# The last layer's output norm moved into its attention, with a new order of the attention's steps

## The chip, the cores and the metric
The kernel runs on one core of one Trainium2 chip. The metric is device time in microseconds (us) of one execution. The core has five engines that matter here: PE (TensorE, matrix products and transposes), ACT (ScalarE), DVE (VectorE), POOL (GpSimd) and SP (SyncE), which issues every DMA in order. They run side by side and wait for each other through semaphores.

## The reference
Two layers of an encoder, for a prompt of 1024 rows (eight tiles of 128) and a sample of 32 rows (tile 8, `SMP`), each row of 1024 features, all in float32.

```
for each layer:
    h = rms_norm(x, g_norm)
    queries, keys, values, gate, index queries/keys/weights = h @ w_in (parts are rotated)
    A: index score = sum over 4 index heads of weight * relu(iq . ik); the 256 best keys a row;
       8 heads of attention over those keys (2 groups of 4 heads)
    B: 4 heads over a window of the last keys, with a sink
    M: 4 heads over 256 memory rows
    x = x + (concat(A, B, M) * silu(gate)) @ w_out
y = rms_norm(x, g_final)
```

The keys and values of each layer are outputs too.

## The kernel before
Python builds one list, `STEPS`, and each engine walks it and issues its own part of each step, so the list is the order of work on every engine. A layer has these stages.

- **Keys and index.** For each tile t: `KEYS` projects, `NORM` transposes the normed rows of tile t+2, `KEYS_T` transposes the keys, and `INDEX` steps score tile t-2. An `INDEX` step before is a pair of index heads on up to 512 keys: two products, each in one half of PE's rows, into a buffer of 1024 columns (L837). ACT applies relu to each half (L1053), and DVE adds each, with its sign, to `bias` (L1320, L1322). There are two score buffers, `score_ps`, and two for transposes, `turn_ps`, used in turn. The sample has 1056 keys, so it takes six steps.
- **Queries and gate**, with the search for the 256th best score in 32 `COUNT` steps on DVE (L1253) and ACT (L969).
- **Attention.** For each tile, four items: B, A group 0, M, A group 1. An item has `QK` steps (scores; DVE adds the mask and takes the maximum, ACT exponentiates, L1099 and L1113), then groups of up to four 128-wide blocks. Two groups make a batch: two `PT` steps (PE transposes the probabilities, L731; ACT, L1124, or DVE, L1444, copies them), then the `PV` products of the batch before. `MIX` (L1460) multiplies by the gate. `OUT` (L746, two halves of 512 columns, 16 records each) projects the mixed tile t-1 during tile t, and `ADD` (L1474) adds it to the residual in `x_sb`, which has two buffers. The order is written out by `attention_steps`; a tile t from 1 to 7 has t+3 batches.
- M scores (and B's of the sample) are read by ACT straight from the score buffer ("direct"); A's and the other B's are first written to SBUF by DVE.
- **Masks.** DVE turns a tile's index scores into a mask in two blocks, `need_of_tile` and `mask_tile`, each beside an `OUT`.
- **The gate's divisors.** From tile 1 on the sums of the softmax are divided out in the gate. `SCALE` (DVE, L1414) makes the reciprocals; SP writes them to DRAM (L682, "norm write"), waits, and loads them back spread over the partitions (L689); POOL multiplies the gate by them (`GATE_SCALE`, L1154); `MIX` waits for that.
- SP's queue in the attention, in order, for t = 1 to 8: norm turn of t for B and M, norm turn of t for A, store of tile t-1 (L696), loads of tile t+1, the residual rows and the gate (L672, L673).
- **The last block**, behind a barrier: all nine tiles are loaded from DRAM, squared and summed on ACT (L1509), mean and power on POOL (L1517, L1520), multiplied on DVE (L1529) and stored.

Of the kernel before, what the change touches and what calls it, by code (L numbers as in the profile page):

```python
# [13 lines left out]
P = 128  # L14
# [36 lines left out]
OUT_AT = [[("A", 0, 1), ("A", 1, 0)], [("A", 0, 1)]]  # L51
# [51 lines left out]
def attention_steps():  # L103


    steps, late, waiting, held, last_mixes = [], [], [], [], []
    last_group = (len(ITEMS) - 1, len(groups_of(ITEMS[-1])) - 1)

    def finish():

        pv = late.pop(0)
        i, g = pv[1:]
        t, kind, kv = ITEMS[i]
        out = [pv]
        if g == len(groups_of(ITEMS[i])) - 1:
            if kind == "M":
                out.append(("MIX", t, 1))
            elif (kind, kv) == ("A", 1):
                out.append(("MIX", t, 0))
        return out  # L120
# [8 lines left out]
    steps += [("EXTRA",)] + score_steps(1)  # L129
    waiting += divisors(score_steps(1)[-1])  # L130
    for i, it in enumerate(ITEMS):
        nxt = score_steps(i + 2) if i + 2 < len(ITEMS) else []
        groups, given = len(groups_of(it)), 0
        t = it[0]
        for g in range(groups):

            if t and it[1:] + (g,) in OUT_AT[t == SMP]:
                c = OUT_AT[t == SMP].index(it[1:] + (g,))
                steps.append(("OUT", t - 1, c))
                if t + 1 in SEARCHED:  # L140
                    steps.append(("MASK", SEARCHED.index(t + 1), c))
                steps.append(("ADD", t - 1, c))
            made = []
            while given < len(nxt) and given * groups <= g * len(nxt):
                steps.append(nxt[given])
                made += divisors(nxt[given])
                given += 1
            if g == groups - 1:
                for q in nxt[given:]:
                    steps.append(q)  # L150
                    made += divisors(q)


            if t == 0 and g == 0:
                steps.append(("DIVIDE", i))
            held.append(("PT", i, g))
            if len(held) == 2 or (i, g) == last_group:
                steps += held
                mixes, last_mixes = last_mixes, []
                steps += mixes  # L160
                while late:
                    for s in finish():


                        (last_mixes if s[0] == "MIX" and s[2] else steps).append(s)
                late += [("PV",) + s[1:] for s in held]
                held.clear()
            if g == 0:
                steps += waiting
                waiting.clear()  # L170
            waiting += made
    steps += last_mixes
    while late:
        steps += finish()
    return steps + [s for t, c in ((NT - 1, 1), (SMP, 0)) for s in (("OUT", t, c), ("ADD", t, c))]
# [9 lines left out]
def index_steps(t):  # L185

    return [("INDEX", t, hp, c) for hp in range(IDX_HEADS // 2) for c in range(-(-NKEYS[t] // 512))]


def plan():  # L190

    steps = [("SQUARE", 0), ("SQUARE", 1), ("NORM", 0), ("NORM", 1)]
    for t in range(TILES):

        index = index_steps(t - 2) if t - 2 in SEARCHED else []
# [59 lines left out]
def copied_by_dve(a):  # L255

    return a % 5 in (1, 3)
# [1318 lines left out]
```

## Time and profile before

| what | value |
|---|---|
| median of 3 runs | 1604.13 us (1602.92 to 1609.43) |
| profiled execution, its own time | 1599.02 us |
| its span | 1597.2 us |
| PE busy | 1400.2 us, 88% |
| DVE busy | 920.6 us, 58% |
| ACT busy | 657.4 us, 41% |
| POOL busy | 155.9 us, 10% |
| mean granted clock of PE | 0.949 |

The span is what the profiler records, and the time is a little longer. Shares are means over stages with different limits, so they are read stage by stage. In the rows, "[1.86 <-DVE hT L1285]" means that the engine was idle for 1.86 us before the instruction, and that DVE's write of `hT` at line 1285 ended the wait. A group "x4" is four records run together; one float32 product of this kernel leaves two records.

### The profile page before, as it was taken

How to read it: one execution, taken by the hardware profiler on the slowest of the kernel's cores; microseconds unless marked ns; L12 is line 12 of the kernel's file. 1: busy time of each engine (PE TensorE's matmuls, PEld its weight loads, DVE VectorE, ACT ScalarE, POOL GpSimd, SP SyncE). 2: the span in 40 equal slices, each digit the busy share in tenths (PEclk: the TensorE clock that was granted, in tenths of full speed). 3: DMA queues.
4: the chain of work that ended last, by engine and by line, in shares of the span. 5: the costliest groups of instructions: out<-in, count | busy, mean ns of one | idle time of the engine just before them, and what ended most of it. 6: DMA issues, size and time to landing. Idle time of an engine off the chain costs nothing. (4 is left out here: it accounts for less than half of the span.)

```text
span 1597.2 us, 19488 instructions
## 1 busy us (share of the span) xinstructions
PE 1400.2 (88%) x6364; PEld 778.1 (49%) x6364; DVE 920.6 (58%) x2527; ACT 657.4 (41%) x1667; POOL 155.9 (10%) x187
## 2 busy tenths in 40 slices
PE   5988799999889999988599887999997999998881
PEld 3444356666545444444344343666664444544450
DVE  1444636887656677655133446488775557676533
ACT  1123526776634433333111334377655333344332
POOL 1100013300001000000011001132000001000003
PEclk9999999999989999999689998999998999999976
DMA  6100410123132312111241004003124222111106
GB/s 200 53 25 21 156 47 1 45 88 94 67 88 73 80 53 54 26 35 29 62 160 52 25 18 161 27 0 119 35 86 133 54 57 57 54 47 53 34 4 247
DMA packets 117960, 108.58 MB, mean 68 GB/s; under 512 B 52368, under 2 KB 90992, under 8 KB 117872
## 3 DMA queue, kind: packets, MB, share of 16 engines
q1 hardware_dynamic: 117872, 107.45, 22.1%
q8 instruction: 51, 0.84, 0.2%
q14 instruction: 37, 0.30, 0.1%
HBM read 81.76 MB, written 25.76 MB: 67 GB/s over the span
## 5 line engine op out<-in xcount | busy, mean ns | idle before, releaser
L746 PE MATMUL score_ps<-w_slot,hT 128*128 128x512 f32 (+2 forms) x1024 | 391.9, 542 | 12.5 <-ACT prob_bm L1053 7.6
L746 PEld LDWEIGHTS score_ps<-w_slot,hT 128*128 128x128 f32 x1024 | 197.7, 196 | 193.3 <-issue 187.3
L746 PE MATMUL score_ps<-w_slot,work 128*128 128x512 f32 x512 | 234.6, 612 | 5.5 <-issue 5.4
L1099 ACT ACTIVATE hT<-hT,neg_top 128x128 f32<-128x128 f32 (+8 forms) x144 | 116.8, 812 | 288.0 <-DVE neg_top L1372 287.8
L1253 DVE TENSOR_SCALAR_CACHE_REDUCE work<-bias,trial 128x384 f32<-128x384 f32 (+3 forms) x256 | 226.1, 883 | 6.9
L969 ACT ACTIVATE work<-bias,neg_trial 128x768 bf16<-128x768 f32 (+2 forms) x192 | 198.4, 1043 | 67.3 <-DVE neg_trial L1249 67.3
L746 PEld LDWEIGHTS score_ps<-w_slot,work 128*128 128x128 f32 x512 | 97.5, 196 | 129.8 <-issue 129.6
L817 PE MATMUL score_ps<-hT,w_slot 128*128 128x352 f32 x448 | 135.2, 460 | 1.4 <-ACT gate_raw L1083 1.4
L731 PE MATMUL turn_ps<-ident,hT 128*128 128x128 f32 (+1 forms) x720 | 98.9, 277 | 27.6 <-ACT work L1124 17.2
L1154 POOL TENSOR_TENSOR work<-work,norm_sb 128x512 f32<-128x512 f32 (+1 forms) x32 | 38.9, 1216 | 855.7 <-DMA norm_sb<-norm_scratch 855.7
L871 PE MATMUL score_ps<-akT,query_mem 64*128 64x512 f32 (+4 forms) x448 | 103.1, 547 | 9.4 <-ACT prob_bm L1113 6.5
L731 PEld LDWEIGHTS turn_ps<-ident,hT 128*128 128x128 f32 (+1 forms) x720 | 74.5, 147 | 74.0 <-issue 33.2
L817 PEld LDWEIGHTS score_ps<-hT,w_slot 128*128 128x128 f32 x448 | 84.8, 190 | 48.4 <-issue 1.7
L1354 DVE CUSTOM_DVE_ANT_0 hT<-score_ps,bias 128x512 f32<-128x512 f32 (+4 forms) x144 | 80.8, 598 | 42.9 <-PE score_ps L871 42.4
L1021 ACT COPY work<-score_ps 128x64 f32<-128x64 f32 (+2 forms) x112 | 20.5, 300 | 179.0 <-PE score_ps L746 179.0
L1124 ACT COPY work<-turn_ps 128x512 f32<-128x512 f32 (+1 forms) x102 | 56.6, 570 | 81.9 <-PE turn_ps L731 81.9
L1474 DVE TENSOR_TENSOR gate_raw<-score_ps,gate_raw 128x512 f32<-128x512 f32 x32 | 22.1, 692 | 118.1 <-PE score_ps L746 118.1
L1320 DVE TENSOR_SCALAR bias<-prob_bm,iw_sign 128x512 f32<-128x512 f32 (+5 forms) x26 | 12.9, 496 | 125.8 <-ACT prob_bm L1053 125.5
L927 PE MATMUL out_a_ps<-work,a_v_sb 128*64 128x256 f32 (+1 forms) x560 | 73.7, 382 | 0.0
L731 PE MATMUL turn_ps<-ident,prob_bm 128*128 128x128 f32 (+2 forms) x280 | 43.3, 286 | 34.3 <-ACT work L1124 24.5
L731 PE MATMUL turn_ps<-ident,work 128*128 128x128 f32 (+1 forms) x284 | 44.3, 292 | 32.8 <-DVE hT L1285 14.9
L1322 DVE SCALAR_TENSOR_TENSOR bias<-prob_bm,iw_sign,bias 128x512 f32<-128x512 f32 (+5 forms) x78 | 51.6, 661 | 29.1 <-ACT prob_bm L1053 26.9
(179 smaller groups left out, 1768.2 us busy)
## 6 DMA issues: line engine op xcount, KB each, us to landing
w_slot<-in_w_in_dram SPq DMA_DIRECT2D x8, 2048.0 KB, 10.3
gate_raw<-in_x_prompt_dram SPq DMA_DIRECT2D x16, 512.0 KB, 3.7
work<-gate_scratch SPq DMA_DIRECT2D x16, 512.0 KB, 4.7
x_scratch<-gate_raw SPq DMA_DIRECT2D x16, 512.0 KB, 4.6
gate_raw<-x_scratch SPq DMA_DIRECT2D x16, 512.0 KB, 3.5
norm_sb<-norm_scratch SPq DMA_DIRECT2D x56, 128.0 KB, 4.1
gate_scratch<-gate_raw SPq DMA_DIRECT2D x16, 264.0 KB, 3.1
gate_scratch<-gate_raw SPq DMA_DIRECT2D x8, 528.0 KB, 2.6
```

Source lines behind the costliest of these rows:

```text
L731: last = nc.tensor.transpose(flat[0:c, pitch * i:pitch * i + r], src, ident[0:r, 0:r])
L746: last = nc.tensor.matmul(out[:, 0:cols], lhs(k), w[:, k, 0:cols], start=(k == 0), stop=(k == KD - 1))
L817: last = nc.tensor.matmul(o, w[:, k, :], hT_v[:, k, THIRD * c:THIRD * (c + 1)], start=(k == 0), stop=(k == KD - 1))
L871: last = nc.tensor.matmul(out[0:r, 512 * u:512 * u + w], aqT[half, head, t * P:t * P + r], akT[half, k0:k0 + w], start=True, stop=True)
L927: last = nc.tensor.matmul(out[HD * u:HD * (u + 1)], v, p.rearrange("p (h n) -> p h n", h=2), start=first and m == 0, stop=final and m == l ...
L969: ins = nc.scalar.activation(signs[c][0:r, 0:NKEYS[t]], bias[0:r, KEY_OFF[t]:KEY_OFF[t + 1]], ACT.Sign, bias=neg_trial[0:r, i:i + 1], accu ...
L1099: ins = nc.scalar.activation(p, p, ACT.Exp, bias=neg, scale=SM_SCALE, accum_out=sums[t % 2][0:r, col:col + 1])
L1124: nc.scalar.copy(prob_t[a % 4][0:w, 0:n], bank.rearrange("p k n -> p (k n)")[0:w, 0:n]).then_inc(free, 1)
L1154: nc.gpsimd.tensor_tensor(gate_sb[t % 2][:, k, 0:r], gate_sb[t % 2][:, k, 0:r], norm_sb[:, k, 0:r], ALU.mult).then_inc(gate_scaled[bm], 1)
L1253: linked(nc.vector.tensor_scalar(tie_a[0:ROWS[t], 0:NKEYS[t]], scored(c), value[0:ROWS[t], c:c + 1], None, ALU.is_ge, ALU.add, accum_out=c ...
L1322: ins = nc.vector.scalar_tensor_tensor(out=s, in0=rl, scalar=sign, in1=s, op0=ALU.mult, op1=ALU.add)
L1354: ins = nc.vector.tensor_tensor_reduce(prob[0:r, head + at:head + at + w], ps[0:r, 512 * u:512 * u + w], bias[0:r, k0 + at:k0 + at + w], 1 ...
```

## The change
- **FINAL.** In the last layer, each prompt tile is normed in place in `x_sb`: `FINAL_RSTD` (ACT squares and sums, POOL makes mean and power) two batches behind the batch of the tile's second `OUT`, and `FINAL` (DVE multiplies by the root and `g_final`) four batches behind. The store of a prompt tile then waits for `FINAL` and writes the output itself. The last block keeps only the sample.
- **Order.** The attention's list is made by batches: scores of an item, one unit a batch, end two batches ahead of its first group where the buffers let them; the second `OUT` comes one batch earlier; masks come in nine parts over several batches. `scalar_order` moves ACT's part of non-direct `QK` steps behind the `PT` copies of the same batch.
- **INDEX.** A step is one index head on all keys of the tile, with one relu and one addition. The sample's last 32 keys go to `out_bm_ps`, and its relu uses the wider `relu_sb`, for which ACT waits until the keys are stored.
- `g_final` gets its own tile, loaded early in the last layer.

```diff
+def batches():
+    groups = [(i, g) for i in range(len(ITEMS)) for g in range(len(groups_of(ITEMS[i])))]
+    return [groups[k:k + 2] for k in range(0, len(groups), 2)]
+def mask_parts(t):
+    return list(range(0 if t in BY_ACT else 3, 9))
+def scores_by_batch(first, last):
+    at, early = [[] for _ in range(last[len(ITEMS) - 1] + 1)], []
+    for i in range(1, len(ITEMS)):
+        units, before = score_steps(i), buffer_of(i)[1]
+        if before is None and first[i] < 2:
+            early += units
+            continue
+        low = 0 if before is None else last[before] + 1
+        for n, unit in enumerate(units):
+            at[max(low, first[i] - 1 - len(units) + n)].append(unit)
+    return early, at
...
+    for t in range(1, TILES):
+        here, prev = ITEMS.index((t, "B", 0)), ITEMS.index((t - 1, "A", 1))
+        out0 = last[prev] + 2
+        out[out0].append(("OUT", t - 1, 0))
+        if t == SMP:
+            continue
+        ahead = next(b for b in range(len(plan)) if ("QK", ITEMS.index((t + 1, "A", 0)), 0) in scores[b])
+        out1 = max(out0, min(ahead, first[ITEMS.index((t, "M", 0))]))
+        out[out1].append(("OUT", t - 1, 1))
+        finals[out1 + 2].append(("FINAL_RSTD", t - 1))
+        finals[out1 + 4].append(("FINAL", t - 1))
...
+    for b, groups in enumerate(plan):
+        steps += out[b] + masks[b] + [("ADD",) + s[1:] for s in out[b]]
+        steps += scores[b]
+        for i, g in groups:
+            if ITEMS[i][0] == 0 and g == 0:
                 steps.append(("DIVIDE", i))
+            steps.append(("PT", i, g))
+        steps += mixes
+        mixes = []
+        for s in products(plan[b - 1]) if b else []:
+            (mixes if s[0] == "MIX" and s[2] else steps).append(s)
+        steps += finals[b] + waiting
+        waiting = [d for q in scores[b] for d in divisors(q)]
+    steps += mixes + waiting + products(plan[-1]) + [s for left in finals[len(plan):] for s in left]
+    return steps + [("OUT", NT - 1, 1), ("ADD", NT - 1, 1), ("FINAL_RSTD", NT - 1), ("OUT", SMP, 0),
+                    ("FINAL", NT - 1), ("ADD", SMP, 0)]
+def scalar_order(steps):
+    order, scores, last = [], [], None
+    for s in steps:
+        if last == "PT" != s[0]:
+            order += scores
+            scores = []
+        if s[0] == "QK" and s[1] and not reads_scores(ITEMS[s[1]]):
+            scores.append(s)
+        else:
+            order.append(s)
+        last = s[0]
+    return order + scores
...
+                    if layer == DEPTH - 1:
+                        sp.dma_start(g_final_sb[:, :], g_final.rearrange("(a n) -> a n", a=1).broadcast_to([P, D_MODEL])
+                                     ).then_inc(final_loaded, 16)
...
                     def x_store(t):
+                        if layer == DEPTH - 1 and t < SMP:
+                            sp.wait_ge(final_made, t + 1)
+                            sp.dma_start(y_prompt[0, t * P:(t + 1) * P, :], x_sb[t % 2][:, :]).then_inc(x_stored[t % 2], 16)
+                            return
...
-                            for u in range(2):
-                                half = slice(HD * u, HD * (u + 1))
-                                last = nc.tensor.matmul(out[0:r, 512 * u:512 * u + w],
-                                                        iqT[half, hp, t * P:t * P + r],
-                                                        ikT[half, k0:k0 + w], start=True, stop=True)
+                            q = iqT[half:half + HD, h // 2, t * P:t * P + r]
+                            for c in range(0, NKEYS[t], 512):
+                                w = min(512, NKEYS[t] - c)
+                                if c < 1024:
+                                    o = out[0:r, c:c + w]
+                                else:
+                                    if h:
+                                        pe.wait_ge(extra_free, h)
+                                    o = out_bm_ps[0:r, 0, 0:w]
+                                last = nc.tensor.matmul(o, q, ikT[half:half + HD, k0 + c:k0 + c + w],
+                                                        start=True, stop=True)
...
-                            for k in range(2):
-                                at = slice(512 * k, 512 * k + w)
-                                ins = nc.scalar.activation(index_relu[u % 2][0:r, at], ps[0:r, at], ACT.Relu,
-                                                           scale=iw_abs[0:r, t, 2 * hp + k:2 * hp + k + 1])
+                            scale = iw_abs[0:r, t, h:h + 1]
+                            ins = nc.scalar.activation(relu[0:r, 0:min(n, 1024)], ps[0:r, 0:min(n, 1024)],
+                                                       ACT.Relu, scale=scale)
...
+                        elif kind == "FINAL_RSTD" and layer == DEPTH - 1:
+                            t = step[1]
+                            for c in range(2):
+                                scores_taken(act, ("OUT", t, c))
+                            if t:
+                                act.wait_ge(final_squared, t)
+                            nc.scalar.activation(final_square[:, :], x_sb[t % 2][:, :], ACT.Square,
+                                                 accum_out=sumsq[:, t:t + 1]).then_inc(final_squared, 1)
...
+                        elif kind == "FINAL" and layer == DEPTH - 1:
+                            t = step[1]
+                            dve.wait_ge(final_rstd, t + 1)
+                            if t == 0:
+                                dve.wait_ge(final_loaded, 16)
+                            x = x_sb[t % 2][:, :]
+                            nc.vector.scalar_tensor_tensor(out=x, in0=x, scalar=rstd[:, t:t + 1], in1=g_final_sb[:, :],
+                                                           op0=ALU.mult, op1=ALU.mult).then_inc(final_made, 1)
...
-                for t in range(TILES):
-                    sp.dma_start(last_x[t][0:ROWS[t], :], x_rows(t)).then_inc(last_loaded[t], 16)
-                for t in range(TILES):
-                    sp.wait_ge(x_added, t + 1)
-                    dst = y_prompt[0, t * P:(t + 1) * P, :] if t < SMP else y_sample[0]
-                    sp.dma_start(dst, last_x[t][0:ROWS[t], :]).then_inc(x_stored[t % 2], 16)
+                sp.dma_start(last_x, x_rows(SMP)).then_inc(last_loaded, 16)
+                sp.wait_ge(x_normed, 1)
+                sp.dma_start(y_sample[0], last_x).then_inc(last_stored, 16)
+                sp.wait_ge(last_stored, 16)
```

## Rows read from the trace of the kernel before

**Rows 1.** The page, part 1: busy time of each engine.
```profile
PE 1400.2 (88%) x6364; PEld 778.1 (49%) x6364; DVE 920.6 (58%) x2527; ACT 657.4 (41%) x1667; POOL 155.9 (10%) x187
```

**Rows 2.** Busy time by stretch: length, PE, PEld, DVE, ACT, POOL, clock, DMA, GB/s.
```profile
97.00:199.00 102.00, 81.39 (x342) 39.75 (x340) 54.40 (x116) 38.63 (x113) 4.02 (x8) 0.92 0.22 71
199.00:430.00 231.00, 227.57 (x840) 142.75 (x841) 159.53 (x488) 137.22 (x292) 36.04 (x36) 0.99 0.17 52
430.00:763.00 333.00, 293.57 (x1599) 154.19 (x1598) 206.43 (x587) 129.52 (x358) 19.42 (x15) 0.96 0.22 57
1243.00:1563.00 320.00, 292.04 (x1602) 152.96 (x1604) 191.21 (x510) 112.83 (x297) 19.03 (x16) 0.96 0.17 45
1565.00:1597.20 32.20, 0.13 (x4) 0.00 (x0) 11.98 (x10) 10.35 (x18) 15.01 (x18) 0.56 0.76 289
```

**Rows 3.** The chain that ended last, its last pieces: start, length, what.
```profile
1569.52 0.36 SPq L1491
...
1573.80 10.64 DMA hT<-x_scratch
...
1584.47 1.16 ACT work L1509 x2
...
1591.01 0.55 POOL rstd L1520
...
1591.64 1.28 POOL meansq L1517
...
1593.58 1.27 DVE gate_raw L1529
```

**Rows 4.** DMA issues: tiles, count, KB each, median us from issue to landing.
```profile
x_scratch<-gate_raw SPq DMA_DIRECT2D x16, 512.0 KB, 4.6
...
norm_scratch<-inv_sum SPq DMA_DIRECT2D x28, 4.0 KB, 9.0
...
gate_raw<-in_x_sample_dram SPq DMA_DIRECT2D x1, 128.0 KB, 2.4
```

**Rows 5.** Timeline of PE between two key projections (layer 0, tile 3's index).
```profile
119.89 1.13 PE L837 MATMUL score_ps<-query_mem 64*128 64x512 f32 x4
...
124.97 1.05 PE L731 MATMUL turn_ps<-ident,work 128*128 128x128 f32 x7 [1.86 <-DVE hT L1285]
...
127.96 0.85 PE L731 MATMUL turn_ps<-ident,work 128*128 128x128 f32 x4 [1.94 <-DVE query_mem L1309]
...
128.60 14.64 PE L746 MATMUL score_ps<-w_slot,hT 128*128 128x512 f32 x32
```

**Rows 6.** Timeline of SP's queue and POOL around tile 2, layer 1.
```profile
1266.29 0.53 SPq L696 DMA_DIRECT2D x_scratch<-gate_raw  x1
...
1270.45 0.34 SPq L672 DMA_DIRECT2D gate_raw<-x_scratch  x1
...
1273.01 0.37 SPq L682 DMA_DIRECT2D norm_scratch<-inv_sum  x1
...
1282.11 1.09 SPq L689 DMA_DIRECT2D norm_sb<-norm_scratch  x2
...
1286.42 1.27 POOL L1154 TENSOR_TENSOR work<-work,norm_sb 128x512 f32<-128x512 f32 x1 [15.87 <-DMA norm_sb<-norm_scratch]
```

**Rows 7.** Timeline of PE: first OUT of tiles 1, 2, 3 and 4, layer 1.
```profile
1272.78 7.10 PE L746 MATMUL score_ps<-w_slot,work 128*128 128x512 f32 x16 [0.41 <-issue]
...
1305.12 7.11 PE L746 MATMUL score_ps<-w_slot,work 128*128 128x512 f32 x16 [0.41 <-issue]
...
1341.36 8.13 PE L746 MATMUL score_ps<-w_slot,work 128*128 128x512 f32 x16
...
1381.87 7.10 PE L746 MATMUL score_ps<-w_slot,work 128*128 128x512 f32 x16 [0.47 <-issue]
```

**Rows 8.** PE's waits from 430 to 765, then 1340 to 1545: total us, times, longest.
```profile
PE turn_ps L731 <- ACT work L1124: 20.3, 15, 2.5
...
PE turn_ps L731 <- ACT work L1124: 15.6, 11, 2.5
```

More of the change, by code:

```diff
@@ new lines, in attention_steps @@
+def attention_steps():
+    plan = batches()
+    first, last = {}, {}
+    for b, groups in enumerate(plan):
+        for i, _ in groups:
+            first.setdefault(i, b)
+            last[i] = b
+    early, scores = scores_by_batch(first, last)
+    out, masks, finals = [[] for _ in plan], [[] for _ in plan], [[] for _ in range(len(plan) + 8)]
+    for t in range(1, TILES):
[9 more added lines that the diff above has]
+        finals[out1 + 4].append(("FINAL", t - 1))
+        if t + 1 in SEARCHED:
+            for k in mask_parts(t + 1):
+                b = first[here] + k if k < 3 else out0 if k < 6 else out1
+                masks[min(b, out0, ahead) if k < 6 else min(b, ahead)].append(("MASK", SEARCHED.index(t + 1), k))
@@ L127, in divisors @@
         return [("SCALE", t, int(kind == "M")), ("GATE_SCALE", t, int(kind == "M"))] if done else []
[L129 to L154, printed above, removed]
-                steps.append(("DIVIDE", i))
[L156 to L175, printed above, removed]
+    def products(groups):
+        made = []
+        for i, g in groups:
+            t, kind, kv = ITEMS[i]
+            made.append(("PV", i, g))
+            if g == len(groups_of(ITEMS[i])) - 1 and kind == "M":
+                made.append(("MIX", t, 1))
+            elif g == len(groups_of(ITEMS[i])) - 1 and (kind, kv) == ("A", 1):
+                made.append(("MIX", t, 0))
+        return made
@@ L193, in plan @@
     for t in range(TILES):
-        index = index_steps(t - 2) if t - 2 in SEARCHED else []
+        index = [("INDEX", t - 2, h) for h in range(IDX_HEADS) if t - 2 in SEARCHED]
         steps += [("SQUARE", t + 2), ("KEYS", t)] + index[0:1] + [("NORM", t + 2)] + index[1:2]
@@ L202, in plan @@
         steps += index[3:4] + [("ROPE", t)]
-    steps += index_steps(NT - 1) + [("KEYS_T", SMP)]
-    last = index_steps(SMP)
+    steps += [("INDEX", NT - 1, h) for h in range(IDX_HEADS)] + [("KEYS_T", SMP)]
     for h, filler in enumerate([("QUERIES", 0), ("MEM", 0), ("MEM", 1)]):
-        steps += [filler] + last[2 * h:2 * h + 2]
-    assert len(last) == 6
+        steps += [filler, ("INDEX", SMP, h)]
+    steps.append(("INDEX", SMP, IDX_HEADS - 1))
     steps += [("TOPK",), ("MEM_T", 0), ("MEM_T", 1)]
@@ L370, in hybrid_stream_kernel @@
         rope_loaded = sem("rope_loaded")
-        last_loaded = [sem(f"last_loaded{t}") for t in range(TILES)]
+        last_loaded = sem("last_loaded")
+        last_stored = sem("last_stored")
+        final_loaded = sem("final_loaded")
         first_sem.clear()
@@ L395, in hybrid_stream_kernel @@
         score_added = sem("score_added")
+        extra_free = sem("extra_free")
         trial_ready = sem("trial_ready")
@@ L960, in _ @@
                     counted = 0
-                    for step in STEPS:
+                    for step in scalar_order(STEPS):
                         kind = step[0]
@@ L1325, in _ @@
-                            if hp == IDX_HEADS // 2 - 1 and 512 * c + w == n and t < SMP:
-                                link(nc.vector.memset(s[0:CHUNK, w - CHUNK:w], NEG))
+                            t, h = step[1:]
+                            r, n = ROWS[t], NKEYS[t]
+                            u = IDX_HEADS * SEARCHED.index(t) + h
+                            if n > 1024:
+                                dve.wait_ge(extra_free, h + 1)
+                            else:
+                                scores_taken(dve, step)
```

168 lines of the change are left out of this document (80 added, 88 removed).

## The prediction

> **What bounds the kernel now.** I read the page first: TensorE (PE) is busy 88% of the span [rows 1]. Then I cut the span by stage, once for the second half of layer 0 and once for layer 1's attention, to see where PE is not the bound [rows 2]. From 199 to 430 us it is busy 227.57 of 231 us, so nothing but PE work counts there. In the key and index stage it is busy 81.39 of 102 us. In the attentions it is busy 293.57 of 333 and 292.04 of 320 us. In the last 32.2 us it does nothing (0.13 us), while ScalarE, GpSimd and VectorE take turns. So there are three places to read closely: the tail, the gaps of the index stage, the gaps of the attention. The chain that ended last [rows 3] shows the tail as a relay: a DMA of 10.64 us, then GpSimd's 1.28 and 0.55 us twice a tile at a step of 2 us, then VectorE's 1.27 us. The waits of PE in the attention are mostly for ScalarE's copy of transposed probabilities (L1124): 20.3 us in 15 waits in layer 0, 15.6 us in 11 waits in the later part of layer 1 [rows 8].
>
> The diff holds five changes, and I cost each.
>
> **1. The tail.** Eight prompt tiles leave the last block, and only the 32-row sample tile stays. Before, PE ends at 1565.13 and the span at 1597.20: 32.1 us. After, counted from the same PE end: tile 7's ADD, Square, mean, power and FINAL run beside the sample's OUT and end about 1 us behind it; then its 512 KB store, 4.6 us [rows 4], in place of the store to scratch of about the same size, and about 0.5 us of barrier: 5.6 us in all. Then one 128 KB load with its issue, 0.5 + 2.4 [rows 4], Square 1.16, mean up to 1.28, power 0.55, the multiply 1.27 [rows 3], and a 128 KB store with its issue, taken as the load's, 2.9 less 0.5 for the lighter direction. That makes 5.6 + 2.9 + 4.3 + 2.4 = 15.2 us, or 14.2 if the mean takes 0.2 rather than 1.28, as it does where GpSimd was idle long before. I take 14.2: **-17.9 us**. Bounds: -14 (a slow barrier and store) to -20.
>
> The work that moves into the attention is 8 Squares (1.16) on ScalarE, 8 means and powers on GpSimd, 8 multiplies (1.27) on VectorE: about 9, 15 and 10 us on engines that are busy 112.83, 19.03 and 191.21 of 320 us [rows 2]. PE waits for none of them directly: I take nothing. If they all stood in front of PE's transposes they would cost 19.
>
> **2. The index scores.** Before, one step multiplies a pair of heads, one in each half of the rows, for 512 keys: four records in 1.13 us [rows 5]. After, one step takes one head over all its keys. A record of 512 columns that has the array to itself takes 7.10 / 16 = 0.44 us [rows 7], so a head over 1024 keys takes 1.78 us where a pair over 512 took 1.13. The trace of before shows the halves overlapping: four records of 0.44 would be 1.78 us end to end. The Trainium skill (TensorEngine Tiling (Array Packing), Key Properties) says that tiles operate independently and can run weight loads and matmuls in parallel, which the 1.13 us bears out; it also speaks against this edit, since one head alone leaves half of the rows idle. Over a layer there are 4 x 5280 = 21,120 head-columns. Alone they take 41.25 x 2 x 0.444 = 36.6 us, paired 20.6 x 1.13 = 23.3 us: +13.3 us of PE work a layer.
>
> But PE waits in this stage, and for the other side of the same edit. Between two key projections (119.89 to 128.60) it sits 1.86 us for VectorE to take the transposed norms and 1.94 us for its key copies [rows 5]; VectorE stood behind a pair of index operations each time. After, ScalarE and VectorE have one wide operation a step. Walking the same stretch with the new steps: first index matmul to 120.75, VectorE's first index operation done at 122.6 rather than 124.1, key transposes at 123.5 rather than 125.0, cache transposes at 125.7, next projection at 127.2 rather than 128.6, so -1.4. The same walk for the other tiles gives -1.4 (384 keys), -1.9 (640), -0.5 (768), -1.1 (896 and 1024, where VectorE is the bound) and, for the sample's 1056 keys, +1.2, since PE is full there and only its small gaps are won. Sum -5.1 a layer, **-10 for two**. Bounds: nothing hidden, +26.6; all but PE's own idle time won (20.6 us a stage [rows 2], less 13.3), -15.
>
> **3. The order in the attention.** ScalarE's softmax passes that read SBUF now stand behind the copies of the same batch, and a memory score (M) no longer shares its batch with the end of a 1024-wide pass. The waits on L1124 then go where only such a pass stood before the copy. Walking the 15 waits of layer 0: seven of group A type (together 5.2 us) and two of group B (2.4) go; eight behind M passes (11.6) shrink to about 3, since M's own 2.6 us on ScalarE stays in front. With some 1 us at the end that is 17 us; VectorE's copies stay behind its score passes and will show in their place, so I take 12 in layer 0 and, for tiles 4 to 8 only, 8 in layer 1: **-20**. Bounds: 0 to -35 (all L1124 waits gone).
> Tile 0 pays: its divisors need passes that ScalarE now does only after the first copy, about 2 us a layer: **+4** (0 to +8).
> Masks move in nine parts. Those beside OUT are covered by its 7.1 us; the three first parts of tiles 5 to 7 are not, 1 us each on VectorE, which has slack: nothing, at worst 4.
>
> **4. The store of a prompt tile now waits for FINAL.** This is where I expect a new wait. SyncE (SP) runs in order: the store of tile t-1, the loads of tile t+1, then the two norm turns of t+1. In layer 1 the store of tile 0 was issued at 1266.29, the load of tile 2 at 1270.45, the first norm write at 1273.01, its load at 1282.11, and the gate multiply came at 1286.42 [rows 6]. After, the store waits for FINAL(0), four batches behind the residual's sum, at the end of the batch of OUT(1,0), about 1283. From there: multiply 1.3, store and issue 4.9, load issues 0.9, norm write with issue 9.3 [rows 4, 6], loads and next write's issue 1.2, second write 9.1, load to multiply 4.3 (1282.11 to 1286.42), multiply 1.3, MIX 0.7: 33 us. That gives OUT(2,0) at about 1315.5 where it was at 1305.12 [rows 7]: +10. OUT(2,0) is followed by its 7.1 us and the batch's rest before FINAL(1), so the cycle from OUT(2,0) to OUT(3,0) is 33 + 10 = 43 us against 36.2: +7. From tile 4 on, FINAL stands in or before the batch ahead of OUT; the chain of 33 us meets a gap of 40.5 us (1341.36 to 1381.87 [rows 7]) and more in each later tile: nothing. With tile 0's shift, **+18**. The reordering gains of tiles 1 to 3 in layer 1 vanish in this wait and are not counted above. Bounds: 0 to +45.
>
> **5. g_final** is loaded early in layer 1 behind the first weights: 512 KB that nothing waits for before FINAL(0). Nothing, at worst 2 us.
>
> **Sum:** -17.9 - 10 - 20 + 4 + 18 = -26 against the profiled execution's 1599.02. The median of before is 5.1 us above that execution, so I make the difference against the median: 1604.1 - 26 = 1578; I say **1577**.
>
> **The rivals.**
> R1, the index cost is not hidden. Place: the L837 matmuls. For it: PE is already busy four fifths of that stage. Against it: the waits of 1.86 and 1.94 us. In full it is +26.6 in place of -10: 1577 + 37 = 1613, slower. It decides from +27 on the sum, which is +8.5 a layer in place of -5. The Trainium skill's page TensorEngine Tiling (Array Packing), section Key Properties, would by itself give this time, since it counts only the lost second half of the rows.
> R2, the store's wait catches every tile. For it: FINAL, store, loads and norm turns lie on one in-order queue. Against it: a norm write has a median of 9.0 us over 28 [rows 4]. If each write took 18 beside the new traffic, the chain would be 51 us and tiles 2 to 6 would miss: about 28 + 25 + 10 + 7 + 3 in place of 17, 1633.
> R3, the order gives nothing (VectorE's copies take ScalarE's place in the waits): 1597.
> R4, the store's wait is covered, because other waits of tiles 2 and 3 fall away with it or the norm writes are quicker: 1559.
>
> **How the numbers follow.** Forecast 0.60 (its own range 1566 to 1590), R1 0.10, R2 0.06, R3 0.12, R4 0.12. The range 1558 to 1598 takes in the forecast, R3 and R4 and leaves out R1 and R2, 0.16. A measurement of this kernel tells about 0.5%, 8 us, from no change. Faster: 0.58 of the forecast's, R4 and half of R3, 0.76. Same: the other half of R3, 0.02 of the forecast's and milder forms of R1 (between +27 and +43 on the sum), 0.14. Slower: the rest of R1 and R2, 0.10.
>
> **What would show it.** The stretch behind the last matmul falls from 32 to 14 or 15 us. The index matmuls no longer overlap, at 1.7 to 1.8 us a step of 1024, while the key stage gets shorter by about 5 us. PE's waits on the L1124 copies in layer 0 fall from 20 us to under 10. In layer 1 PE idles before OUT(2,0) and OUT(3,0), 10 us or so each, behind GpSimd's gate multiply, and before no later OUT. Layer 0's attention gets shorter and layer 1's up to OUT(3,0) longer. I am wrong if the key stage grows, if a long wait stands before OUT(4,0) or later, or if layer 0's attention keeps its length.

## The result and the profile after

The changed kernel is slower. Its median is 1656.51 us (1654.22 to 1658.28, 4 runs) against 1605.07 us before (1602.92 to 1609.43, 4 runs): ratio 1.0324, 95% interval 1.0308 to 1.0341, +51 us where -26 was forecast. The profiled span grew from 1597.2 to 1655.6 us, +58.4. The page's first part, for [rows 1]:

```profile
PE 1451.4 (88%) x6364; PEld 804.4 (49%) x6364; DVE 902.0 (54%) x2479; ACT 654.2 (40%) x1627; POOL 147.6 (9%) x187
```

I cut both spans at the same events of PE's timeline. "Key stages" is from the key projection at 84.6 us (layer 0), or from layer 1's first, to the start of query projection 1. "Start" is from the last gate product to the first `OUT`. "Attention" is from the first `OUT` to the sample's last product. The later runs are cut in the same way (us):

| kernel | key stages, layer 0 + 1 | start, 0 / 1 | attention 0 | attention 1 | tail | span |
|---|---|---|---|---|---|---|
| before | 148.0 + 211.1 | 30.6 / 30.5 | 320.9 | 322.0 | 32.1 | 1597.2 |
| changed | 152.5 + 210.4 | 38.7 / 38.4 | 337.1 | 362.7 | 13.2 | 1655.6 |
| e1 early divisors | 146.9 + 215.7 | 38.6 / 38.8 | 304.8 | 335.3 | 13.2 | 1596.0 |
| e2 new index alone | 147.8 + 210.4 | 30.5 / 30.5 | 324.7 | 321.7 | 31.9 | 1599.5 |
| e3 FINAL alone | 148.1 + 213.5 | 30.6 / 30.5 | 321.9 | 363.4 | 13.1 | 1623.2 |
| e9 early, store later | 146.7 + 215.5 | 35.2 / 35.2 | 308.3 | 318.4 | 13.2 | 1575.7 |
| e11 the same, ACT by the list | 146.8 + 215.6 | 35.1 / 35.3 | 325.4 | 328.6 | 13.3 | 1602.9 |
| e12 changed, store later | 152.5 + 215.4 | 38.9 / 38.7 | 332.5 | 346.1 | 13.4 | 1639.6 |
| e14 e9, tile 0 as before | 152.5 + 215.6 | 26.4 / 26.4 | 307.1 | 317.5 | 13.4 | 1560.3 |

The tail fell as forecast, from 32.1 to 13.2 us. Nearly everything between grew (layer 1's key stage did not), layer 0's attention too, which holds no `FINAL`. Code that is the same in two kernels does not take the same time in each: layer 0's attention of before took 320.9 us, and 324.7 with e2's edit, which leaves it as it was. So differences of a few us in one stretch are not resolved. The same stretches as windows of before (columns as in [rows 2]):

```profile
461.50:782.40 320.90, 292.95 (x1638) 153.59 (x1636) 189.77 (x508) 112.90 (x297) 19.87 (x16) 0.97 0.18 46
1243.20:1565.10 321.90, 293.94 (x1636) 153.93 (x1636) 191.04 (x508) 112.83 (x297) 19.03 (x16) 0.96 0.18 46
```

and of after:

```profile
474.00:811.10 337.10, 295.24 (x1634) 155.22 (x1632) 187.29 (x504) 113.03 (x295) 18.70 (x16) 0.94 0.18 44
1279.70:1642.40 362.70, 299.97 (x1634) 156.07 (x1632) 195.99 (x511) 121.11 (x311) 24.58 (x32) 0.91 0.17 40
```

PE's waits in the two attentions of after (total, times, longest):

```profile
PE score_ps L788 <- issue: 14.0, 5, 6.9
PE score_ps L788 <- DVE work L1529: 13.1, 2, 7.9
PE score_ps L918 <- ACT prob_bm L1168: 5.9, 6, 2.9
...
PE score_ps L788 <- DVE work L1529: 24.8, 3, 10.9
PE score_ps L788 <- issue: 17.9, 4, 7.6
```

The waits for ACT's copies, 20.3 us in [rows 8], are gone (0.9 us in each layer's attention). In their place PE waits 27.1 us before `OUT` (L788) in layer 0 and 42.7 us in layer 1, for `MIX` (L1529). Before the long ones `MIX` waits for the gate, and the gate for the norm turns. One tile of layer 0 of before, all engines, by time:

```profile
491.12 7.10 PE L746 MATMUL score_ps<-w_slot,work 128*128 128x512 f32 x16 [0.41 <-issue]
491.12 0.20 DVE L1414 RECIPROCAL inv_sum<-sums 128x8 f32<-128x8 f32 x1
...
504.20 0.20 DVE L1414 RECIPROCAL inv_sum<-sums 128x8 f32<-128x8 f32 x1
...
504.43 0.37 SPq L682 DMA_DIRECT2D norm_scratch<-inv_sum  x1
...
513.42 1.09 SPq L689 DMA_DIRECT2D norm_sb<-norm_scratch  x2
...
518.51 1.27 POOL L1154 TENSOR_TENSOR work<-work,norm_sb 128x512 f32<-128x512 f32 x1 [10.84 <-DMA norm_sb<-norm_scratch]
...
522.67 0.69 DVE L1460 TENSOR_TENSOR work<-out_a_ps,work 128x512 f32<-128x512 f32 x1 [1.65 <-PE out_a_ps L927]
```

and of after, a tile of layer 0 whose first `OUT` had begun at 508.85:

```profile
521.15 0.20 DVE L1483 RECIPROCAL inv_sum<-sums 128x8 f32<-128x8 f32 x1
...
521.38 0.37 SPq L720 DMA_DIRECT2D norm_scratch<-inv_sum  x1
...
533.41 0.19 DVE L1483 RECIPROCAL inv_sum<-sums 128x8 f32<-128x8 f32 x1
...
534.01 0.59 SPq L720 DMA_DIRECT2D norm_scratch<-inv_sum  x1
...
543.10 1.08 SPq L727 DMA_DIRECT2D norm_sb<-norm_scratch  x2
...
547.67 1.26 POOL L1225 TENSOR_TENSOR work<-work,norm_sb 128x512 f32<-128x512 f32 x1 [9.81 <-DMA norm_sb<-norm_scratch]
...
549.02 0.69 DVE L1529 TENSOR_TENSOR work<-out_a_ps,work 128x512 f32<-128x512 f32 x1 [7.05 <-POOL work L1225]
```

Before, the reciprocals (`SCALE`) of the next tile come 0 and 13.1 us after the tile's first `OUT` starts, and the second gate multiply 27.4 us after it; it ends 2.9 us ahead of `MIX`, which waits for the products alone. After, they come 12.3 and 24.6 us after `OUT`, and `MIX` follows the gate multiply directly. The chain is no slower; it begins 12 us later. The cause stands in the list: `waiting` gives out a batch's divisors only at the end of the next batch. The list of before held them back as well, but its M score came a batch earlier (two to three batches for tiles 4 to 7). So for tile 2 `SCALE` of B and M moves from ahead of `OUT` (1, 0) to ahead of `OUT` (1, 1), and `SCALE` of A to a batch after that.

For tiles 5 and 6 of layer 1 the gate is not what `MIX` waits for:

```profile
1493.37 1.26 POOL L1225 TENSOR_TENSOR work<-work,norm_sb 128x512 f32<-128x512 f32 x1 [6.76 <-DMA norm_sb<-norm_scratch]
...
1494.98 0.55 POOL L1216 TENSOR_TENSOR rstd<-meansq,half_neg 128x1 f32<-128x1 f32 x1
1495.64 1.28 DVE L1538 SCALAR_TENSOR_TENSOR gate_raw<-gate_raw,rstd,g_final_sb 128x1024 f32<-128x1024 f32 x1 [6.20 <-POOL rstd L1216]
...
1499.57 0.68 DVE L1529 TENSOR_TENSOR work<-out_a_ps,work 128x512 f32<-128x512 f32 x1
```

In GpSimd's order the power for `FINAL` stands behind the gate multiply. DVE stands 6.20 us in `FINAL` for it, and `MIX`, behind `FINAL` on DVE, comes 4.9 us after the gate was ready (3.5 us for tile 6). The waits before these two `OUT`s are 7.6 and 3.3 us.

### The profile page after: what moved, and what is told of

Read it like the earlier page. It is cut to its first block and busy times, and to the rows that moved or that the text cites. A ratio compares the mean times of both kernels' runs of the same rounds, so it can differ in the third digit from the quotient of the medians.

```text
span 1655.6 us, 19388 instructions
## 1 busy us (share of the span) xinstructions
PE 1451.4 (88%) x6364; PEld 804.4 (49%) x6364; DVE 902.0 (54%) x2479; ACT 654.2 (40%) x1627; POOL 147.6 (9%) x187
## 5 line engine op out<-in xcount | busy, mean ns | idle before, releaser
L788 PE MATMUL score_ps<-w_slot,hT 128*128 128x512 f32 (+2 forms) x1024 | 387.4, 537 | 5.5 <-DMA w_slot<-in_w_in_dram 5.0
L788 PE MATMUL score_ps<-w_slot,work 128*128 128x512 f32 x512 | 253.1, 652 | 69.9 <-DVE work L1529 37.9
L788 PEld LDWEIGHTS score_ps<-w_slot,hT 128*128 128x128 f32 x1024 | 195.4, 194 | 185.6 <-issue 179.7
L788 PEld LDWEIGHTS score_ps<-w_slot,work 128*128 128x128 f32 x512 | 104.8, 210 | 204.8 <-issue 204.6
L773 PE MATMUL turn_ps<-ident,hT 128*128 128x128 f32 (+1 forms) x720 | 94.5, 271 | 14.9 <-DVE hT L1503 11.9
L885 PE MATMUL score_ps<-query_mem 64*128 64x512 f32 (+2 forms) x192 | 94.2, 676 | 0.5 <-ACT prob_bm L1104 0.4
L1068 ACT COPY work<-score_ps 128x64 f32<-128x64 f32 (+2 forms) x112 | 20.5, 297 | 175.7 <-PE score_ps L788 175.7
L918 PEld LDWEIGHTS score_ps<-akT,query_mem 64*128 64x128 f32 (+1 forms) x448 | 35.8, 182 | 71.4 <-ACT prob_bm L1168 29.1
L1168 ACT ACTIVATE prob_bm<-score_ps,neg_top 128x256 f32<-128x256 f32 (+2 forms) x80 | 36.1, 460 | 79.3 <-DVE neg_top L1464 79.1
L1104 ACT ACTIVATE prob_bm<-score_ps,iw_abs 128x384 f32<-128x384 f32 (+5 forms) x48 | 41.4, 863 | 49.2 <-PE score_ps L885 45.5
```

What stands on the lines that cost most here:

```text
L773: last = nc.tensor.transpose(flat[0:c, pitch * i:pitch * i + r], src, ident[0:r, 0:r])
L788: last = nc.tensor.matmul(out[:, 0:cols], lhs(k), w[:, k, 0:cols], start=(k == 0), stop=(k == KD - 1))
L885: last = nc.tensor.matmul(o, q, ikT[half:half + HD, k0 + c:k0 + c + w], start=True, stop=True)
L918: last = nc.tensor.matmul(out[0:r, 512 * u:512 * u + w], aqT[half, head, t * P:t * P + r], akT[half, k0:k0 + w], start=True, stop=True)
L1104: ins = nc.scalar.activation(relu[0:r, 0:min(n, 1024)], ps[0:r, 0:min(n, 1024)], ACT.Relu, scale=scale)
```

## The experiments

Each ratio is to the kernel before, on the same chip, with its 95% interval.

**e1, early divisors.**
```diff
-        steps += finals[b] + waiting
-        waiting = [d for q in scores[b] for d in divisors(q)]
+        steps += finals[b] + [d for q in scores[b] for d in divisors(q)]
```


> The changed kernel with one edit: a batch's divisors (SCALE and GATE_SCALE) stand at the end of the batch that holds their last score, not at the end of the next batch. Theory: the new list asks for the divisors so late that two norm turns of about 11 us each, one behind the other in SP's queue, end after the first OUT of each tile could start. In the changed kernel PE waits 27 us before OUT products in layer 0 (14.0 and 13.1) and 43 us in layer 1 (24.8 and 17.9). With both turns about one batch earlier, 5 to 10 us a tile, most of this goes in both layers: 35 to 60 us less, 1600 to 1620. Rival, the store's wait for FINAL is what delays the norm turns: then layer 0, which has no FINAL, would have no such wait, and this edit gains nothing in layer 1, since SP would still sit at the store; at most 16 us less, 1640.

Measured: 1600.28 us, 0.9944 (0.9920 to 0.9969), against 1.0324 of the changed kernel: about 61 us for one batch's hold. The edit does not bring the M score back to its old batch; it takes away the hold behind it. Both attentions gave back much the same, 32.3 and 27.4 us. PE's waits in layer 0's attention:

```profile
PE score_ps L917 <- ACT prob_bm L1167: 5.9, 6, 2.6
PE score_ps L787 <- issue: 5.8, 5, 1.7
```

The waits before `OUT` fell from 27.1 to 6.6 us (5.8 and one of 0.8). The rest of the 32.3 us is mostly PE's busy time, 295.24 to 285.55 us for the same records. In layer 1, 30 us more than in layer 0 were left.

**e2, the new index alone**, in the kernel before.


> The kernel before with the index scores of the changed one (one head over all keys) and nothing else. My forecast was 10 us less, 1595. Read from the changed kernel's trace, the start of the second query projection moved by +4.5 us in layer 0 and the same stage of layer 1 by -1.0 us: 3 us more, 1608. Rival, the cost of the unpaired heads in full: 26.6 us more, 1631.

Measured: 1612.1 us, 1.0021 (0.9974 to 1.0067). No gain, and not the full cost either; the forecast's -10 us lies outside the interval.

**e3, FINAL alone**, in the kernel before: its own list with the two steps put in.
```diff
+            due += [(n + 6, ("FINAL_RSTD", s[1])), (n + 10, ("FINAL", s[1]))]
+    return steps[:-4] + tail[:2] + [("FINAL_RSTD", NT - 1), tail[2], ("FINAL", NT - 1), tail[3]]
```


> The kernel before with FINAL, the store's wait for it and the short last block, and nothing else of weight: the list of the kernel before, with FINAL put in two and four batches behind the second OUT; ACT follows the list; the index scores as before. Theory of the late divisors: with the old list the divisors are early enough, the store's wait costs 0 to 10 us, and the tail of 17 us is gained: 1587 to 1597. Rival, the store's wait itself delays each norm turn: the 22 us by which layer 1's attention grew more than layer 0's in the changed kernel stay, 1609.

Measured: 1626.63 us, 1.0108 (1.0075 to 1.0140). My expectation was wrong and the rival's too small. Without the new list, the store's wait costs twice the tail's gain: attention 1 took 363.4 us against 321.9 in layer 0. One tile, SP, DVE, POOL and PE by time:

```profile
1290.04 1.27 DVE L1546 SCALAR_TENSOR_TENSOR gate_raw<-gate_raw,rstd,g_final_sb 128x1024 f32<-128x1024 f32 x1
...
1291.34 0.36 SPq L753 DMA_DIRECT2D out_dram<-gate_raw  x1
...
1294.45 0.34 SPq L730 DMA_DIRECT2D gate_raw<-x_scratch  x1
...
1295.31 0.58 SPq L740 DMA_DIRECT2D norm_scratch<-inv_sum  x1
...
1306.68 1.09 SPq L747 DMA_DIRECT2D norm_sb<-norm_scratch  x2
...
1307.82 0.59 SPq L740 DMA_DIRECT2D norm_scratch<-inv_sum  x1
...
1313.08 1.12 PE L989 MATMUL out_bm_ps<-prob_t,b_v_sb 128*64 128x256 f32 x4 [5.29 <-DVE work L1537]
...
1317.70 1.08 SPq L747 DMA_DIRECT2D norm_sb<-norm_scratch  x2
...
1322.44 1.26 POOL L1232 TENSOR_TENSOR work<-work,norm_sb 128x512 f32<-128x512 f32 x1 [10.20 <-DMA norm_sb<-norm_scratch]
```

The next `OUT` waited 10.4 us, to 1324.59. From `FINAL` to `OUT` it is 34.5 us, where the forecast's chain has 33. The wait of 5.3 us before it, for the first `MIX`, was not in the forecast. The steps between first `OUT`s were 48.3, 49.4 and 47.5 us for tiles 2, 3 and 4 against 32.3, 36.2 and 40.5 before: +16, +13 and +7.

**e4, the changed kernel with the list of before** (and ACT by the list).


> The changed kernel with the attention's list of the kernel before (FINAL put in two and four batches behind the second OUT) and ACT in the order of that list; the new index scores and FINAL stay. So it is the changed kernel less its order. Theory of the late divisors: all of the loss of layer 0 and most of layer 1's goes, and the time is that of the other two parts, the kernel before less 17 for the tail, plus 3 for the index, plus 0 to 10 for the store: 1591 to 1601. Rival, the store or the index sets the time: above 1625.

Measured: 1626.09 us, 1.0086 (1.0056 to 1.0116). It equals e3, so beside `FINAL` the new index costs nothing that shows; the new order is what made the changed kernel slower than this.

**e5, early divisors and a changed queue.**
```diff
                             ).then_inc(norm_written[bm], 16)
+                        if t >= 2 and not bm:
+                            x_store(t - 2)
+                            rows_load(t)
                         sp.wait_ge(norm_written[bm], 16 * t)
...
-                        x_store(t - 1)
                         if t + 1 < TILES:
-                            tile_load(t + 1)
+                            gate_load(t + 1)
```


> The kernel of the run with the early divisors, with one edit to SP's queue: a tile's store (which waits for FINAL) and the load of the residual rows two tiles on stand between the norm write and the loads of the next tile's second norm turn, where SP waits some 9 us for the write anyway; the load of the gate goes ahead alone. Theory, the store's wait is what is left: with the early divisors layer 1's attention behind its first OUT lasted 335 us against 305 in layer 0, which has no FINAL. These 30 us go: 1570, ratio to the kernel before 0.976. Rival, FINAL's own work on ACT, GpSimd and VectorE fills that difference: no change, 1600.

Measured: 1609.65 us, 1.0009 (0.9986 to 1.0032), 9 us slower than e1. The difference between the layers fell from 30 to 10 us (attention 1 329.1, attention 0 319.4), but attention 0 grew by 15. SP's queue in layer 0 shows why:

```profile
543.70 0.36 SPq L726 DMA_DIRECT2D norm_scratch<-inv_sum  x1
544.16 0.53 SPq L747 DMA_DIRECT2D x_scratch<-gate_raw  x1
555.55 0.35 SPq L712 DMA_DIRECT2D gate_raw<-in_x_prompt_dram  x1
556.00 1.09 SPq L736 DMA_DIRECT2D norm_sb<-norm_scratch  x2
```

The residual load waits for the store, and the store, issued right behind the norm write, took 11.4 us; in e3's layer 1, with no write ahead of it, SP went on after 3.1 us (the first output store, to another tensor). The second turn so takes 12.3 us from write to loads, where the first takes 8.5.

**e6, FINAL alone with that queue.**


> The kernel before with FINAL and the short last block (the run of that name), with the same edit to SP's queue. Theory of the store's wait: layer 1's attention took 363 us against 322 in layer 0, the 41 us go, 1585, ratio 0.985, the kernel before less its tail. Rival, FINAL's own work: 1626.

Measured: 1587.07 us, 0.9872 (0.9831 to 0.9914). In this list the turns have slack for the slower second one, so all of the store's wait went. In this list FINAL's own work on ACT, GpSimd and VectorE costs nothing measurable: attention 1 took 321.2 us, attention 0 325.6, and VectorE waits before none of the `FINAL` steps of tiles 0 to 6.

**e7, e5 with tile 0 in order on ACT.**
```diff
-        if s[0] == "QK" and s[1] and not reads_scores(ITEMS[s[1]]):
+        if s[0] == "QK" and ITEMS[s[1]][0] and not reads_scores(ITEMS[s[1]]):
```


> The kernel with the early divisors and the changed queue, and ACT takes tile 0's scores in the order of the list. Theory: in the changed kernel the stretch from the last gate product to the first OUT grew by 7 to 8 us in each layer, because tile 0's divisors are made on VectorE from sums that ACT now makes only behind a copy. With the list's order 4 to 7 us a layer come back: 8 to 14 less than the same kernel without the edit, about 1560. Rival, it is the list itself (the products of two more score steps ahead of the first transposes): no change from that kernel.

Measured: 1600.44 us, 0.9932 (0.9910 to 0.9953), 9 us less than e5. The starts fell from 39.2 and 38.8 to 35.7 and 35.2 us; some 5 us a layer were still left over the 30.6 and 30.5 of before.

**e8, the changed kernel with e5's queue.**


> The changed kernel with the edit to SP's queue alone; the divisors stay late. If the two causes add, layer 1's attention falls from 360 us to the 337 of layer 0, 22 less, 1634, and the waits before OUT of layer 0 stay at 27 us. If the late divisors are the whole cause, 1656.

Measured: 1688.86 us, 1.0508 (1.0472 to 1.0544). Both expectations were wrong. With late divisors there is no slack, so the longer second turn, 12 to 14 us, lies on the way to `OUT` in both layers (attentions 362.2 and 368.8 us; waits before `OUT` 42.5 and 45.5 us).

**e9, e7 with the store behind both turns.**
```diff
-                        if t >= 2 and not bm:
-                            x_store(t - 2)
-                            rows_load(t)
...
                             gate_load(t + 1)
+                        if t >= 2:
+                            x_store(t - 2)
+                            rows_load(t)
```


> The kernel of the last run but with a tile's store and its residual load behind both norm turns of the next tile, not between the second turn's write and its loads (early divisors, tile 0 in order, as there). In that run the second turn took 12 to 14 us from write to loads where the first took 8.5, since SP also waited for the store to land; layer 0's attention behind its first OUT took about 317 us against 305 with the early divisors and the old queue. Theory: with the store out of the turn, 305 in both layers and 3.6 less at each start: 24 less, about 1575, ratio 0.98. Rival, the store's traffic slows whichever norm write is next and moves with it: no change, 1600.

Measured: 1578.63 us, 0.9818 (0.9779 to 0.9858), near the 1575 expected; but the 305 us came in layer 0 alone (308.3), and layer 1 took 318.4. The two as windows:

```profile
465.80:774.10 308.30, 290.14 (x1634) 153.53 (x1632) 187.75 (x502) 112.92 (x295) 19.06 (x16) 0.97 0.21 48
1244.10:1562.50 318.40, 293.53 (x1632) 154.53 (x1632) 197.78 (x510) 121.09 (x311) 24.69 (x32) 0.96 0.19 45
```

Part of the 10 us between the layers is `FINAL` on VectorE: for tiles 4 and 5 it stands there 3.11 and 2.50 us for GpSimd's power, ahead of the next tile's `MIX`, and the waits before `OUT` of tiles 5 and 6 are 4.5 and 2.5 us, against 0.8 and 0.5 in layer 0. No run moved that step, so its full price is open.

**e10, FINAL alone with this queue.**


> The kernel before with FINAL, the short last block and the same queue (store and residual load behind both turns of the next tile). With the store between write and loads it was 1587, and layer 0's attention 326 us against 322 of the kernel before. Theory: 322 in both layers, 0 to 8 less, 1579 to 1587. Rival, a residual load that comes too late for ADD: above 1590.

Measured: 1588.19 us, 0.9878 (0.9834 to 0.9922), the same as e6.

**e11, e9 without ACT's own order.**
```diff
-                    for step in scalar_order(STEPS):
+                    for step in STEPS:
```


> The first kernel of this call with ACT in the order of the list throughout (no scores moved behind the copies). The attention behind layer 0's first OUT was 16 us shorter with the new list, early divisors and ACT's order than in the kernel before. If ACT's order carries that gain, as my forecast had it (20.3 us of waits for ACT's copies), this run is 15 to 30 us slower than the first; if the list carries it, within 5.

Measured: 1601.51 us, 0.9953 (0.9931 to 0.9976): 23 us slower than e9. The waits for ACT's copies are back, in layer 0's attention:

```profile
PE turn_ps L782 <- ACT work L1196: 14.3, 11, 3.5
```

ACT's order carries the gain: 325.4 to 308.3 us in attention 0, 328.6 to 318.4 in attention 1. The list alone, 325.4, gains nothing on the 320.9 of before.

**e12, the changed kernel with e9's queue.**


> The changed kernel with this queue alone, so with the late divisors and without the store's wait ahead of the norm turns. If the two causes add, layer 1's attention (360 us) falls to the 337 of layer 0: 22 less, 1634. If the late divisors are the whole cause, 1656.

Measured: 1638.97 us, 1.0180 (1.0138 to 1.0222). Attention 1 fell by 16.6 us, attention 0 by 4.6. That is what the same edit to the queue is worth with early divisors (16.9 us from e1 to e9), so the two causes add, as the first expectation had it. The key stage of layer 1 was 5 us longer, in code that is the same.

**e13, e9 with the old index.**


> The fastest kernel so far (early divisors, ACT in the order of the list for tile 0, a tile's store and residual load behind both norm turns of the next tile) with the index scores of the kernel before. My forecast for the index alone was 10 us in favour of the new one. The stage it stands in took 358 to 363 us for both layers in the runs with the new index and 359 to 364 with the old. Theory: no difference, within 4 us of that kernel's 1579. Rival, my forecast: 10 us more, 1589.

Measured: 1573.65 us, 0.9778 (0.9746 to 0.9810); e9 had 0.9818. The intervals overlap, and my forecast's gain of 10 us is not there.

**e14, e9 with tile 0's DIVIDE steps ahead.**
```diff
-        steps += scores[b]
+        steps += [("DIVIDE", i) for i, g in groups if ITEMS[i][0] == 0 and g == 0 and i > 1]
+        steps += scores[b] + ([] if b else [("DIVIDE", 1)])
         for i, g in groups:
-            if ITEMS[i][0] == 0 and g == 0:
-                steps.append(("DIVIDE", i))
             steps.append(("PT", i, g))
```
(`DIVIDE` 0 goes behind the score of tile 0's M item.)


> The same fastest kernel with the four DIVIDE steps of tile 0 ahead of the scores of their batch, as near as may be to the list of the kernel before; nothing else. From the last gate product to the first OUT it takes 35.2 us a layer, where the kernel before takes 30.6 and the changed kernel 38.7, and 3.5 of the 8 have come back with ACT's order. Theory, VectorE makes the divisors behind score passes that nobody waits for yet: 2 to 4.6 us a layer come back, 4 to 9 in all, 1570 to 1575. Rival, ACT's place for tile 1's first scores: no change, 1579.

Measured: 1557.8 us, 0.9692 (0.9660 to 0.9725), the fastest of all and faster than both kernels of this case. The start is 26.4 us in each layer, 8.8 less than e9's and less than the 30.6 of before; I had expected at most 4.6. In the changed kernel PE waits for the divisions of tile 0 four times:

```profile
445.38 1.11 PE L773 MATMUL turn_ps<-ident,prob_bm 128*128 128x128 f32 x4 [2.12 <-DVE prob_bm L1503]
449.88 1.11 PE L773 MATMUL turn_ps<-ident,hT 128*128 128x128 f32 x4 [3.39 <-DVE hT L1503]
...
458.29 1.97 PE L773 MATMUL turn_ps<-ident,prob_bm 128*128 128x128 f32 x8 [2.49 <-DVE prob_bm L1503]
...
465.91 1.12 PE L773 MATMUL turn_ps<-ident,hT 128*128 128x128 f32 x4 [2.57 <-DVE hT L1503]
```

Of these 10.6 us 1.05 are left in e14.

**e15, e14 with the old index.**


> The kernel with the DIVIDE steps ahead, with the index scores of the kernel before. Theory, the index makes no difference: ratio 0.969, within 0.4% of the kernel without the edit (0.9692). Rival A, my forecast, the new index is worth 10 us: 0.975. Rival B, the new index costs 5 us, as the run before hinted (0.9778 against 0.9818): 0.966 or less.

Measured: 1569.14 us, 0.9758 (0.9731 to 0.9785), 0.7% slower than e14. Here the new index is worth 10 us, in e13 against e9 it cost 6, and alone (e2) it was worth nothing. But what separates e15 from e14 lies outside the key stages (363.7 us against 368.1): e15's starts were 27.6 us each and its attentions 311.2 and 324.8, 13.8 us more than e14's in all, in code that is the same. So the index's own effect is smaller than what such stretches differ by from kernel to kernel; why they differ is not shown.

## Why the prediction was wrong

The span's +58.4 us, by the forecast's terms:

| term | forecast | measured | from |
|---|---|---|---|
| tail | -17.9 | -18.9 | changed |
| index, both layers | -10 | +3.8 (358 to 368 us in eleven kernels with the new, 359 to 365 in six with the old) | key stages |
| order in the attention | -20 | -20 (-16.1, and -3.6 with what `FINAL` and its store still cost) | e1, e9 against before |
| tile 0 | +4 | +16.0 | starts |
| store waits for FINAL | +18 | +16.9 (alone, old list: +41) | e1 less e9; e3 |
| late divisors | none | +59.7 (32.3 and 27.4) | changed less e1 |

With 0.7 us between the layers this sums to 58.5.

**The step that failed is the third, "The order in the attention".** It follows ACT's passes and PE's waits and takes the place of `SCALE` as given. The diff moved the divisors a batch back in the early tiles, and the chain behind them (write, loads, gate multiply, two turns in line) was about 3 us from being the bound in the early tiles. The forecast worked that chain out for the store, 33 us, and never laid it from `SCALE`'s new place, so the late divisors stand in the sum with nothing. e1 shows their price: one change to the list, about 61 us. The forecast had a rival with waits before every `OUT` (R2), but with the wrong mechanism, slow norm writes behind the store. The writes took 8.6 to 11.8 us to their loads; it was the start of the chain that had moved, in layer 0 as well.

**The order's own gain was right.** The L1124 waits went, ACT's order is what removed them (e11), and in layer 0 the size is near: 16.1 us against 12, with the divisors early. Layer 1's 3.6 us against 8 is not a clean measure: it is within what equal code differs by, and `FINAL`'s cost lies in it (layer 1 took 10 us more than layer 0 in e9). That the table's row comes to the forecast's -20 is luck.

**The store's wait was right in place and chain and mis-sized.** In e3 the waits before `OUT` of tiles 2 and 3 were 10.4 and 8.1 us, where I had 10 and 7. Left out were the wait for the first `MIX` (5.3 and 3.1 us), the slower products behind each wait (9.88 and 9.08 us for 7.1), and tile 4: 41 us in place of 17 (the 18 less tile 0's shift). "From tile 4 on nothing" was wrong by 7 and a few more.

**FINAL's own work was put at nothing.** That held in the list of before (e6). In the new list VectorE stands in `FINAL` for 6.20, 3.35 and 4.46 us for tiles 4 to 6 of the changed kernel, ahead of the next tile's `MIX` for the first two. The forecast counted the busy time of these steps and not the place of GpSimd's power behind the gate multiply.

**Index.** The walk held for the first tiles: in the changed kernel the key projections of tiles 5 and 6 start 1.4 and 3.6 us sooner, counted from the one at 84.5. It failed at the end of the stage, where PE ran near its lower level (1.2 GHz). A head of tile 6, 896 keys, took 1.77 us at 176.16 and 3.35 at 181.96:

```profile
176.16 1.77 PE L885 MATMUL score_ps<-query_mem 64*128 64x512 f32 x4
...
181.96 3.35 PE L885 MATMUL score_ps<-query_mem 64*128 64x512 f32 x4
...
186.93 3.35 PE L885 MATMUL score_ps<-query_mem 64*128 64x512 f32 x4
```

From 180 to 205 us the granted clock was 0.57, before 0.80; PE was busy 24.55 us of the 25 there, before 17.77. The forecast priced every head at the full clock. What the clock does here differs from kernel to kernel with the same code: from 120 to 150 us it was 0.86 in the changed kernel and 1.00 in e9, and layer 0's key stage took 152.5 and 146.7 us. So the +3.8 is not the index's price alone. R1, the cost in full (+26.6), did not come true either. Whether the new index is worth a few microseconds in one list or another stays open: the three pairs gave +3, +6 and -10 us.

**Tile 0** was mis-sized: 16 us for 4. ACT's order makes 7 of them (e7), the divisions' place on DVE more than the rest (e14).

**The tail**: right, 13.2 us against 14.2. Three slips in the working change nothing: the tail's first pieces add to 6.1 us and not 5.6, seven, two and eight waits make 17 and not 15, and R1 comes to 1614.

## What to carry to other kernels

When a list of steps is written anew, lay every chain through DMA from its new start to its consumer, tile by tile, and compare with the slack it had; a step of 0.2 us that starts such a chain is worth more care than the passes around it. A layer without the new work (here layer 0) is a control in the same trace: what grows there has another cause. A short step that waits for another engine delays all that stands behind it on its own. In an in-order DMA queue, work that waits on a late engine goes behind the latency chain, not into its wait.

## What the runs showed of the hardware

A 512 KB store issued 0.5 us behind a 4 KB norm write kept SP 11.4 us (e5), against 3.1 us with no write ahead (e3). The medians from issue to landing say the same for each kind of store: 11.5 us (e5) against 4.6 (e3) to scratch, 11.3 against 2.7 to the output. So here the small write delays the large store. The Trainium skill, DMA: Bandwidth & Descriptors, section Queues, rings and completion order, says that each DMA engine takes its descriptors in ring order. The rows fit that; no run here shows the order itself.

A wait can cost more than its length. In the changed kernel PE stood for 10.9 us before an `OUT`; the windows of that wait and of the `OUT`, with the granted clock as third column from the end:

```profile
1349.50:1360.40 10.90, 0.00 (x1) 0.01 (x1) 2.80 (x9) 4.31 (x14) 1.95 (x3) 0.52 0.19 24
1360.40:1369.10 8.70, 8.67 (x18) 3.72 (x20) 2.92 (x5) 0.00 (x0) 0.05 (x1) 0.82 0.00 0
```

In the wait the granted clock was 0.52, about the 1.2 GHz level, and the 16 records behind it took 8.6 us in place of 7.1. Late divisors cost 20.5 us of waits and 9.7 us of PE busy time in layer 0. The forecast left that out.

In the changed kernel a single head over 512 keys took 1.12 us in two records (at 117.52 us), as long as a pair in four, 1.13 us [rows 5]: the second half of the rows cost nothing there.
